# Attention with rows of 64 per head, the least of negated scores, four score slots, and a pair's first head ahead of the second

## What is computed

```python
qa, ka, va, qb, kb, vb = jnp.split(p, cuts, axis=-1)      # 8 + 2 + 2 + 8 + 8 + 8 heads of 64
# group A: a window of +-128 tokens, 8 query heads over 2 key heads, and a sink logit
s_loc = jnp.where(valid, einsum(qi, ki) * scale, NEG_INF)
p = softmax(concatenate([s_loc, s_ctx, s_sink], axis=-1))
# group B: a clamped neighbourhood of 8 x 16 on the 16 x 64 grid, with a bias
s = where(mask, einsum(qr, kblk) * scale + bias, NEG_INF)
p = softmax(concatenate([s, s_ctx], axis=-1))
o = einsum(p_loc, v) + einsum(p_ctx, vc)                  # both groups
```

## Time and profile before

| | |
|---|---|
| median of 3 runs | 2629.34 us |
| profiled execution | 2639.0 us |
| its span, first to last instruction | 2637.1 us |
| PE busy in it | 2436.6 us, 92% |
| DVE, ACT, POOL busy | 1894.8, 1502.1, 389.1 us |
| granted TensorE clock, mean | 0.964 |

### The profile page before, as it was taken

One profiled execution on the slowest core, in us unless ns is written; L12 is line 12 of the kernel. 1 busy time (PEld: TensorE's weight loads), 2 busy tenths in 40 slices (PEclk: granted clock), 3 DMA queues, 4 the chain that ended last, 5 costly groups with the idle time before them and its releaser, 6 DMA issues. The chain is left out here.

```text
span 2637.1 us, 36689 instructions
## 1 busy us (share of the span) xinstructions
PE 2436.6 (92%) x12074; PEld 1869.4 (71%) x12074; DVE 1894.8 (72%) x2591; ACT 1502.1 (57%) x1899; POOL 389.1 (15%) x297
## 2 busy tenths in 40 slices
PE   7999978888779569999999999999999999999987
PEld 2466557777667458787877778788888888888862
DVE  2550437787757578888898888877868777777866
ACT  3210037677643266777777777656656656666752
POOL 1000012222112110202021010102111211210210
PEclk8999989999978689999999999999999999999998
DMA  9751044343243189989898999979878878878988
GB/s 350 149 152 64 0 113 101 81 95 81 67 163 118 41 324 314 362 307 366 306 362 316 351 327 339 331 252 326 287 257 318 305 242 312 320 247 295 338 302 318
DMA packets 296053, 639.51 MB, mean 243 GB/s; under 512 B 12146, under 2 KB 13394, under 8 KB 295810
## 3 DMA queue, kind: packets, MB, share of 16 engines
q1 hardware_dynamic: 277970, 571.29, 62.8%
q0 software_dynamic: 18000, 67.13, 7.2%
HBM read 599.69 MB, written 44.65 MB: 244 GB/s over the span
## 5 line engine op out<-in xcount | busy, mean ns | idle before, releaser
L1808 DVE TENSOR_TENSOR w_lo_x<-wring,w_hi_x 128x2048 fp32r<-128x2048 f32 x444 | 1008.7, 2285 | 53.2 <-ACT w_hi_x L1649 22.0
L1649 ACT ACTIVATE w_hi_x<-wring 128x2048 fp32r<-128x2048 f32 x444 | 843.0, 1911 | 46.9 <-DMA wring<-in_w_mlp 46.3
L2020 PE MATMUL psum<-w_hi_x,x_hi_x 128*128 128x512 f32 x992 | 417.4, 421 | 10.2 <-DVE w_lo_x L1808 10.2
L2022 PE MATMUL psum<-w_hi_x,x_lo_x 128*128 128x512 f32 x992 | 389.2, 392 | 0.0
L2021 PE MATMUL psum<-w_lo_x,x_hi_x 128*128 128x512 f32 x992 | 388.2, 391 | 0.0
L2017 PE MATMUL psum<-w_hi_x,x_both_x 128*128 128x512 f32 x640 | 270.8, 423 | 0.0
L1612 POOL TENSOR_TENSOR poolgate_x<-poolgate_x 128x1 f32<-128x1 f32 x61 | 66.0, 1082 | 1261.4 <-DVE y_x L1853 831.2
L2018 PE MATMUL psum<-w_lo_x,x_both_x 128*128 128x512 f32 x640 | 250.7, 392 | 0.0
L2020 PEld LDWEIGHTS psum<-w_hi_x,x_hi_x 128*128 128x128 f32 x992 | 188.7, 190 | 45.8 <-DVE w_lo_x L1808 12.5
L2022 PEld LDWEIGHTS psum<-w_hi_x,x_lo_x 128*128 128x128 f32 x992 | 187.0, 188 | 41.8
L2021 PEld LDWEIGHTS psum<-w_lo_x,x_hi_x 128*128 128x128 f32 x992 | 187.9, 189 | 36.5
(11 more groups left out here) (328 smaller groups left out, 3916.2 us busy)
## 6 DMA issues: line engine op xcount, KB each, us to landing
wring<-in_w_mlp SPq DMA_DIRECT2D x444, 1024.0 KB, 6.2
bias<-bias_d SPq DMA_DIRECT2D x32, 640.0 KB, 7.9
late<-in_w_ada SPq DMA_DIRECT2D x32, 512.0 KB, 3.8
yg<-y_d SPq DMA_DIRECT2D x32, 512.0 KB, 6.9
ring<-in_w_ada SPq DMA_DIRECT2D x4, 2048.0 KB, 8.6
ring<-in_w_in SPq DMA_DIRECT2D x4, 2048.0 KB, 9.8
ring<-in_w_out SPq DMA_DIRECT2D x2, 2048.0 KB
mix_d<-o SPq DMA_DIRECT2D x16, 256.0 KB, 4.4
```

Of the source, the lines that this page charges most:

```text
L1649: act.activation(w_hi[:, u % HI, k, :], ring[:, u % RING, k, :], ACT.Copy).then_inc(hi_done, 1)
L1808: dve.tensor_tensor(w_lo[:, u % LO, k, :], ring[:, u % RING, k, :], w_hi[:, u % HI, k, :].bitcast(F32), ALU.subtract).then_inc(lo_done, 1)
L2020: pe.matmul(bank, hi[:, k, :], w_hi[:, u % HI, k, :], start=(not biased and k == 0), stop=False)
L2022: last = pe.matmul(bank, lo[:, k, :], w_hi[:, u % HI, k, :], start=False, stop=(k == KD - 1))
```

## The change

- A key head's 64 rows now hold one part: `K.ka[:, low, :]` and `K.kb[:, 2 j + low, :]` with low 0 for the high part and 1 for the remainder. Partitions 0 to 63 are one head, 64 to 127 the other of a pair. ScalarE copies the high part of both heads at once and VectorE makes one remainder.
- A pair of group A is now heads a and a + 4, one for each key head; of group B two neighbours. `qh` and `ql` hold 8 pairs instead of 16 heads. q is split in two pieces of 128 partitions a tile, one for each group.
- A score stretch takes three products over 64 rows instead of two over 128: qh with the keys' high part, qh with their remainder, ql with the high part. All of the first head's stand ahead of the second's.
- The scores of a pair are made together, two pairs ahead of its transposes, when both masks of the pair before are done (`s_masked`).
- `S` has 4 slots. The mask instruction multiplies by -1 and takes the least; the exponential has scale -1 and the least as its bias. The negation is gone; for group B the context's least is the start value of the second instruction.
- VectorE's order is mask of 2p + 2, copy of 2p, mask of 2p + 3, copy of 2p + 1; the q remainder stands at the end of pair 3 and pair 7 of a tile.

```diff
-                    for half in range(2):
-                        last = act.activation(key_part(g, half, HIGH), ps[HD * half:HD * half + HD, bank, 0:width], ACT.Copy)
-                    last.then_inc(group_copied, 1)
+                    act.activation(key_part(g, 0), ps[:, bank, 0:width], ACT.Copy).then_inc(group_copied, 1)
...
-        qh, ql = sb("qh", [P, NH, P], F32R), sb("ql", [P, NH, P], F32R)
+        qh, ql = sb("qh", [P, PAIRS, P], F32R), sb("ql", [P, PAIRS, P], F32R)
-        S = sb("S", [P, 2, LB + CTX])
+        S = sb("S", [P, SLOTS_S, LB + CTX])
...
-                for to, kv in parts:
-                    for q in (qh, ql):
-                        last = pe.matmul(flat[:, to], q[:, s, :], kv, start=(q is qh), stop=(q is ql))
-                last.then_inc(s_done, 1)
+                for half in range(2):
+                    flat = ps[:, 2 * half:2 * half + 2, :].rearrange("p b n -> p (b n)")
+                    for to, here, width in parts:
+                        for n, (q, low) in enumerate(((qh, 0), (qh, 1), (ql, 0))):
+                            last = pe.matmul(flat[:, to:to + width], q[HD * half:HD * half + HD, at, :], key(low, half, slice(here, here + width)), start=(n == 0), stop=(n == 2))
+                    last.then_inc(s_done, 1)
...
+            scores(0)
+            scores(1)
+            for pair in range(ALL // 2):
+                transposes(2 * pair)
+                if pair >= 2:
+                    to_rows(pair - 2)
+                if pair:
+                    values(pair - 1)
+                transposes(2 * pair + 1)
+                if pair + 2 < ALL // 2:
+                    scores(pair + 2)
...
-                act.activation(S[:, s % 2, 0:keys(s, i)], S[:, s % 2, 0:keys(s, i)], ACT.Exp, bias=negm[:, s:s + 1], accum_out=den[:, s:s + 1]).then_inc(p_done, 1)
+                act.activation(row, row, ACT.Exp, bias=least[:, s:s + 1], scale=-1.0, accum_out=den[:, s:s + 1]).then_inc(p_done, 1)
...
+                evacuate(2 * pair + 1)
+                if ahead:
+                    probs(2 * pair + 3)
+                if at == A_PAIRS - 1:
+                    act.wait_ge(sinkd_done, i + 1)
+                    act.activation(sinke[:, :], sinkd[:, :], ACT.Exp).then_inc(sinke_done, 1)
+                if i + 1 < T and at == A_PAIRS - 1:
+                    query(2 * i + 2)
+                if i + 1 < T and at == PAIRS - 1:
+                    query(2 * i + 3)
...
-                    link(dve.tensor_tensor_reduce(S[:, s % 2, 0:every], flat[:, 512 - local:512 + CTX], mask_a[:, 0:every], 1.0, sink[:, s:s + 1], ALU.add, ALU.max, mx[:, s, 0:1]))
-                    dve.tensor_scalar(negm[:, s:s + 1], mx[:, s, 0:1], -1.0, None, ALU.mult).then_inc(s_masked, 1)
+                    dve.tensor_tensor_reduce(row[:, 0:every], flat[:, 512 - local:512 + CTX], mask_a[:, 0:every], -1.0, sink[:, s:s + 1], ALU.add, ALU.min, least[:, s:s + 1]).then_inc(s_masked, 1)
...
+                if ahead:
+                    mask(2 * pair + 2)
+                evacuate(2 * pair)
+                if ahead:
+                    mask(2 * pair + 3)
+                evacuate(2 * pair + 1)
...
+                if i + 1 < T and at == A_PAIRS - 1:
+                    remainder(2 * i + 2)
+                if i + 1 < T and at == PAIRS - 1:
+                    remainder(2 * i + 3)
```

More of the change, by code:

```diff
@@ L540, in rotated @@
                     link(dve.tensor_tensor(rot[:, 0, :], rot[:, 0, :], rot[:, 1, :], ALU.add))
[L541 to L546, removed]
+                    link(dve.tensor_copy(key_part(g, 0), rot[:, 0, :]))
+                    last = dve.tensor_tensor(key_part(g, 1), rot[:, 0, :], key_part(g, 0).bitcast(F32), ALU.subtract)
                 last.then_inc(rope_done, 1)
@@ L559, in _ @@
                     dve.wait_ge(group_copied, g + 1)
-                    for half in range(2):
-                        last = dve.tensor_tensor(key_part(g, half, LOW), ps[HD * half:HD * half + HD, g % 4, 0:width], key_part(g, half, HIGH).bitcast(F32), ALU.subtract)
-                    last.then_inc(k_low, 1)
+                    dve.tensor_tensor(key_part(g, 1), ps[:, g % 4, 0:width], key_part(g, 0).bitcast(F32), ALU.subtract).then_inc(k_low, 1)
                 for m in range(2 * (g - FIRST_PIECE), 2 * (g - FIRST_PIECE) + 2):
@@ L708, in on_scalar, with q_part @@
             return min(512, keys(s, i) - P)
[L710 to L717, removed]
+        def q_part(n):
+            i, group = divmod(n, 2)
+            return slice(A_PAIRS * group, A_PAIRS * group + A_PAIRS), (K.qa, K.qb)[group][:, :, i * P:i * P + P]
         block = ctx.enter_context(nc.Block())
@@ L838, in to_rows @@
                 pe.wait_ge(ot_copied, pair + 1)
-                group, at = divmod(pair, GROUP_PAIRS)
+                group, at = divmod(pair, A_PAIRS)
                 if at == 0:
@@ new lines, in evacuate @@
+            def evacuate(h):
+                i, s = divmod(h, NH)
+                act.wait_ge(pt_done, h + 1)
+                act.activation(PT[:, h % PROBS, 0:on_scalar(s, i)], ps[:, 4, 0:on_scalar(s, i)], ACT.Copy).then_inc(pt_low, 1)
+            query(0)
+            query(1)
+            probs(0)
+            probs(1)
+            for pair in range(ALL // 2):
+                i, at = divmod(pair, PAIRS)
+                ahead = pair + 1 < ALL // 2
+                evacuate(2 * pair)
+                if ahead:
+                    probs(2 * pair + 2)
+                if pair:
+                    copy_values(pair - 1)
+                evacuate(2 * pair + 1)
[8 more added lines that the diff above has]
+                    query(2 * i + 3)
@@ L912, in _, with remainder @@
             link = linker(dve, dve_own)
-            def remainder(first, n, start, made):
-                part, to, heads, source = q_piece(first, n)
-                dve.wait_ge(q_high, made)
-                dve.tensor_tensor(ql[to, heads, :], source[part, :, bass.ds(start, P)], qh[part, heads, :].bitcast(F32), ALU.subtract).then_inc(q_low, 1)
-            def mask(s, i, at):
-                dve.wait_ge(s_done, at + 1)
+            def remainder(n):
+                to, source = q_part(n)
+                dve.wait_ge(q_high, n + 1)
+                dve.tensor_tensor(ql[:, to, :], source, qh[:, to, :].bitcast(F32), ALU.subtract).then_inc(q_low, 1)
@@ new lines, in _ @@
+            link(dve.tensor_scalar(sink[:, :].rearrange("p (a e) -> p e a", e=2), sink_in[:, :].rearrange("p (e a) -> p e a", e=2), -1.0, None, ALU.mult))
+            mask(0)
+            mask(1)
+            remainder(1)
+            for pair in range(ALL // 2):
+                i, at = divmod(pair, PAIRS)
+                ahead = pair + 1 < ALL // 2
+                if ahead:
+                    mask(2 * pair + 2)
+                evacuate(2 * pair)
+                if ahead:
+                    mask(2 * pair + 3)
+                evacuate(2 * pair + 1)
+                if at == 1 and i:
+                    output(i - 1, 1)
+                if at == A_PAIRS + 1:
+                    output(i, 0)
+                if i + 1 < T and at == A_PAIRS - 1:
+                    remainder(2 * i + 2)
+                if i + 1 < T and at == PAIRS - 1:
+                    remainder(2 * i + 3)
```

184 lines of the change are left out of this document (67 added, 117 removed).

## The result

The changed kernel takes 2609.82 us (median of 4 runs, 2605.1 to 2612.9) against 2629.46 for the kernel before (4 runs): ratio 0.9925, 95% interval 0.9905 to 0.9945. The forecast was 2620, faster by 9.6; measured are 19.6.

The account below looks back on a forecast made before the run. No engine was full; waits in the attention's ring bounded the kernel, TensorE next. 274.8 + 43.6 + 5.8 + 14.5 = 338.7 against 348.3 us, so -9.6: median 2619.7, taken as 2620; range 2602 to 2652.

Parts of the forecast that it names:

- The ring: Attention loop of mask, exponential, transposes, copy, next mask; four S slots were to remove the bulk of 73.5 us of waits.
- the sum: Attention's forecast length: TensorE's need 274.8, third products 43.6, switches net 5.8, waits 14.5, giving 338.7 against 348.3 us.
- The 73.5 us of before: Attention time beyond TensorE's need of 274.8 in 348.3 us: waits, short drains and a slow clock at the start.
- the collisions: VectorE's q remainders held up by GpSimd's bias additions in the attention; the first tile lost two such waits.
- The stalls for the masks at the two remainders: Scores waiting for masks queued behind VectorE's q remainders: 0.9 and 0.5, so 1.4 us a tile, 9.8 in seven tiles.
- the overlap of the two heads: In a pair's scores, the second head's first product may run beside the first's last: 0.11 a pair, 7.0 us.
- The switches: Array shape changes around the scores: two more a pair, 128 in all, 0.1 us each, 12.8 us; bounds 0 to 0.2.
- The layout by itself: Scores over 64 rows: three products for two add 43.6 us, switches less overlap a net 5.8.
- Weights are loaded under a product: Score products; the rival that loads can't overlap in half the rows: 0.11 more each, 95 us, 2715; chance 0.06.
- The collision: Rival: at the tile's end the neighbourhood remainder lands behind GpSimd's addition, 20 to 35 us lost, 2640 to 2655; chance 0.17.
- No change: Rival: switches around the scores cost 0.2 us each, the sum is 12.8 higher, 2632 us; chance 0.15.
- Heads side by side: Rival: both heads' score products run beside each other, 70 us saved, some 40 given back by the ring, 2580; chance 0.06.

Follow-up runs that it names:

- ring_later_pieces: Kernel before's layout in the new order, three score slots, no GpSimd additions, VectorE's q pieces a pair later: attention 291.7 us, against 336.9 with early pieces.
- apart: Changed kernel, with TensorE waiting for the first head's score products to finish before the second head's start: 2652.79 us, 1.0078 of the kernel before.
- late_remainder: Changed kernel with VectorE's neighbourhood q remainder moved behind the second mask of the next tile's first pair: 2622.01 us, 0.9968 of the kernel before.
- two_products: Changed kernel without the product of q's high part with the keys' remainder: 2572.81 us, 0.9777 of the kernel before.

## Why the prediction was right, and where it was off

- **The sign and the bound held.** The ring moved the waits from TensorE to the other engines, and TensorE's own work decides. Its need before, 274.8 in the sum, is borne out: in *ring_later_pieces* the spacings of starts, with the waits taken out, add up to 273 (an estimate: each stage of work counted at the tenth percentile of its form).
- **The waits were sized well, in sum.** The 73.5 us of before are 19.1 of additions (348.3 - 329.2), 37.5 that the order takes (329.2 - 291.7) and 16.9 that stay over the old layout (291.7 - 274.8). The sum let 14.5 stay; in the changed kernel the same estimate gives TensorE 309, so 13 stay of 322.0. But the sum put "the bulk" to the ring and named the collisions only for tile 0; a quarter of the 73.5 was theirs. Less what the layout costs, the ring brings 8.5, and two thirds of the measured gain are the collisions that went. The stalls for the masks at the two remainders were oversized: 1.4 a tile, 9.8 in all, and the idle time ahead of scores is 3.4 us (2.9 in the row above, 0.5 in the other forms). In that sum TensorE's way adds up to 5.6, or 5.7 with a switch, not to 5.9.
- **The mis-sized term is the overlap of the two heads.** The step that failed is "the second head's first product may run beside the first head's last one": 0.11 a pair. By *apart* it is 0.43; 64 x 0.32 = 20.5. The argument against running side by side was that a head's products stand together in the queue. The trace shows that this keeps them apart only up to the first head's last three.
- **The switches were undersized, which worked the other way.** Forecast 0.1 each. Behind the values as in the earlier trace rows, seven transposes to the first score product take 0.91 here (529.27 to 530.18), where the old layout took 0.74. Behind the scores, where the rows above have 0.21 to the next transposes, the old layout in the new order has 0.12 (timeline of *ring_later_pieces*):

```profile
496.60 0.28 PE L819 MATMUL psum<-kbT,ql 128*128 128x256 f32 x1
496.72 0.71 PE L838 MATMUL psum<-ident,S 128*128 128x128 f32 x5
```

  The first product behind a switch also stands longer ahead of its successor than there: 0.02 for scores, 0.06 for transposes (medians of single records). Together that is 0.34 a pair for two switches, 21.8 us where the sum has 12.8. It took the start of a score product behind a transpose for 0.11 without a switch; the trace of before has 0.03.
- **How these add up.** The attention was put at 338.7 and took 322.0, 16.7 less: 20.5 more of overlap, 9.0 more for switches, some 2 less of waits, and 2.9 for a smaller slip, which makes some 16. The slip: the sum counts the scores of the first two pairs, 24 products of some 0.12, though they run ahead of the first transposes, where the measured stretch starts. The layout by itself was put at 43.6 + 5.8 = 49.4 and costs 29.0 in the table. That difference holds the same overlap and switches, and besides them waits that differ between the two corners, so it is no second measure of the overlap.
- **A product over 64 rows takes as long as one over 128**, as taken: 0.17 for 384 keys.
- **Weights are loaded under a product**, also within one half of the rows:

```profile
530.18 0.29 PEld L797 LDWEIGHTS psum<-kaT,qh 64*128 64x128 f32 x2 [0.17 <-issue]
530.47 0.18 PEld L797 LDWEIGHTS psum<-kaT,ql 64*128 64x128 f32 x1
```

  The load for the first head's third product runs from 530.47 to 530.65, while the second runs, and the third follows 0.17 after the second. The rule of the Trainium skill ("TensorE: Matmul & The Clock Gate", Part 3, "The mechanism") would have made this 95 us longer; this trace disagrees for products of one row group.
- **The rivals.** The collision did not come at the tile's end, but by margins of 0.29 to 1.00 us; *late_remainder* shows that it is real and what it costs, and the sink's subtraction met one in tile 0. "No change" asked for switches of 0.2; they are 0.17 in the mean, so that rival was nearly right in its cause, and only the overlap kept it from coming true. Heads side by side, put at 0.06, is in part the case, and with the products in turns it is 2581.84. The 2580 of that rival is no result of its own terms: 2620 - 70 + 40 is 2590.
- **Interior tiles** were to take 44 to 45 us and take 42.3: eight pairs with 0.3 more of overlap, 0.14 more for switches, and some 0.9 a tile less of stalls.
- **Still open:** the attention became 26.3 us shorter, the medians differ by 19.6. The missing 6.7 would lie in the other stages, of which the later ones alone vary by 11 us between profiles; two of the four runs took 2605.1 and 2606.8, two 2612.9. No run here tells what sets this. That the forecast of 2620 came within 10.2 us is in part luck: the attention alone was mis-sized by 16.7, itself a net of misses in both directions.

## What to carry to other kernels

Where products use half of the array's rows, put those of the two halves in turns in the program: the edit of a few lines was worth 28 us here in the medians (23.8 in the attention), more than the whole change. When waits are to be removed, first take away the one suspected collision and look what is left; here a quarter of the idle time had nothing to do with the ring that the profile suggested. The sign of a collision is one instruction that takes several times what the same line and shape take elsewhere. And the price of an edit depends on the order around it (45.8 or 29.0 us for the same layout), so measure both corners before adding up.

## What was not expected of the hardware

A product of the second head starts before products of the first that stand ahead of it in the program: 530.648 against 530.816, 530.934 and 531.050, and in the 896-key pair 524.998 with three of the first head's nine still to come (525.102, 525.270 and 525.389). They differ in the half of the rows. The Trainium skill ("TensorE: Matmul & The Clock Gate", Part 2, "Step-by-step: what each phase is for") has products in program order and only weight loads pulled ahead; as the profile records starts, that does not hold here for products of different halves. How far ahead it reaches is the same throughout these traces: with four, six or nine products a head, in the changed kernel and in *two_products*, the other head's first product starts with three of the first's still to come, in all 112 pairs that can be told apart. What sets the three no run shows.
